# Small products and fillers in another order, other bank rings, and the LayerNorm's affine step spread over two engines, in a hybrid trunk kernel

## What is computed

```python
for layer in range(DEPTH):                       # DEPTH = 2
    mix = _even_mixer(x, ...) if layer % 2 == 0 else _odd_mixer(x, ...)
    x = _layer_norm(ALPHA * x + mix, ln1_g[layer], ln1_b[layer])
    x = _layer_norm(ALPHA * x + _swiglu(x, ...), ln2_g[layer], ln2_b[layer])

def _layer_norm(x, g, b):                        # over the last axis
    xc = x - mean(x)
    return xc * rsqrt(mean(xc * xc) + LN_EPS) * g + b

# gated linear attention, chunks of 64 tokens: the masked product within a chunk
attn = where(causal, einsum('bhcid,bhcjd->bhcij', q_g, k_g), 0.0)
o_intra = einsum('bhcij,bhcjv->bhciv', attn, vc)
# odd layer: gated RMSNorm of the delta rule's output
o = _rms_norm(o) * norm_g * silu(gate)
```

## Time and profile before

| | us |
|---|---|
| median of 3 runs | 1285.34 |
| lowest and highest | 1285.04, 1287.56 |
| the profiled execution | 1283.91 |
| its span | 1282.1 |
| TensorE busy | 1250.3 |
| VectorE, ScalarE, GpSimd busy | 462.7, 432.9, 598.9 |

### The profile page before, as it was taken

How to read it: one execution, slowest core, us unless ns; L and a number is a source line. 1 busy time by engine, 2 the same in 40 slices (tenths; PEclk the granted TensorE clock), 3 DMA queues, 4 the chain that set the end, 5 groups by cost and what they waited for, 6 DMA issues and landing times.

```text
span 1282.1 us, 16970 instructions
## 1 busy us (share of the span) xinstructions
PE 1250.3 (98%) x7104; PEld 1027.5 (80%) x7104; DVE 462.7 (36%) x763; ACT 432.9 (34%) x600; POOL 598.9 (47%) x286
## 2 busy tenths in 40 slices
PE   9999999999999999998999999999999999999997
PEld 7878877888888888886777878887788888888885
DVE  5548945211111000115687955553521101010105
ACT  4174623322222221224453355452422222221111
POOL 4241243964444443445743346364595444435341
PEclk9999999999999999999999999999999999999999
DMA  9321032333333233231344342022233333324221
GB/s 305 99 67 66 1 115 84 99 99 99 98 99 99 83 121 125 99 96 49 98 110 124 99 100 92 26 67 99 66 99 99 99 99 99 99 82 134 80 99 65
DMA packets 109375, 122.98 MB, mean 96 GB/s; under 512 B 22386, under 2 KB 84148, under 8 KB 109300
## 3 DMA queue, kind: packets, MB, share of 16 engines
q1 hardware_dynamic: 101828, 118.59, 29.4%
q10 hardware_dynamic: 7472, 3.31, 1.0%
HBM read 117.96 MB, written 3.70 MB: 95 GB/s over the span
## 4 chain that ended last, share of the span: by engine, by line
PE 86%; DVE 7%; POOL 3%; issue 3%; DVEq 1%; ACT 1%; ACTq 0%; POOLq 0%
PE bank L1562 26%; PE bank L1563 26%; PE bank L1564 26%; PE bank L1893 3%; POOL w_lo L638 2%; DVE f_ab L1083 1%; DVE KH L1355 1%; DVE OO L1333 1%; DVE SS L1331 1%; PE bank L1608 1%; DVEq L435 1%; PE bank L1721 0%; PE bank L1845 0%; DVE x_tm L1106 0%; PE bank L1782 0%
## 5 line engine op out<-in xcount | busy, mean ns | idle before, releaser
L638 POOL TENSOR_TENSOR w_lo<-w_raw,w_hi 128x1024 fp32r<-128x1024 f32 (+1 forms) x200 | 470.0, 2374 | 495.3 <-ACT w_hi L768 495.3
L1562 PE MATMUL bank<-x_hi,w_hi 128*128 128x512 f32 x928 | 364.3, 393 | 7.5 <-DVE f_ab L1083 4.0
L1564 PE MATMUL bank<-x_hi,w_lo 128*128 128x512 f32 x928 | 361.7, 390 | 0.0
L1563 PE MATMUL bank<-x_lo,w_hi 128*128 128x512 f32 x928 | 361.6, 390 | 0.0
L768 ACT ACTIVATE w_hi<-w_raw 128x1024 fp32r<-128x1024 f32 (+1 forms) x200 | 196.3, 1031 | 218.3 <-issue 167.3
L1562 PEld LDWEIGHTS bank<-x_hi,w_hi 128*128 128x128 f32 x928 | 174.6, 188 | 46.9 <-issue 8.4
L1564 PEld LDWEIGHTS bank<-x_hi,w_lo 128*128 128x128 f32 x928 | 174.5, 188 | 36.6
L1563 PEld LDWEIGHTS bank<-x_lo,w_hi 128*128 128x128 f32 x928 | 174.5, 188 | 35.4
L1150 DVE TENSOR_TENSOR f_ab<-bank,f_ab 128x512 f32<-128x512 f32 x44 | 30.4, 691 | 368.9 <-PE bank L1564 368.9
L1563 PE MATMUL bank<-w_lo,h_hi 128*128 128x512 f32 x352 | 140.4, 399 | 0.0
L1562 PE MATMUL bank<-w_hi,h_hi 128*128 128x512 f32 x352 | 138.7, 394 | 0.0
(11 more groups left out here) (270 smaller groups left out, 1179.5 us busy)
## 6 DMA issues: line engine op xcount, KB each, us to landing
w_raw<-ffn_w_gate_dram SPq DMA_DIRECT2D x22, 1024.0 KB, 5.3
w_raw<-ffn_w_up_dram SPq DMA_DIRECT2D x22, 1024.0 KB, 5.3
w_raw<-ffn_w_down_dram SPq DMA_DIRECT2D x20, 1024.0 KB, 5.0
w_raw<-od_w_in_dram SPq DMA_DIRECT2D x16, 1024.0 KB, 5.9
w_raw<-ev_w_in_dram SPq DMA_DIRECT2D x8, 1024.0 KB, 5.9
w_raw<-ev_w_out_dram SPq DMA_DIRECT2D x4, 1024.0 KB, 5.1
w_raw<-od_w_out_dram SPq DMA_DIRECT2D x4, 1024.0 KB, 5.1
x_fm<-x_fm_dram SPq DMA_DIRECT2D x8, 256.0 KB, 6.7
```

The lines of the kernel that those rows point to most:

```text
L638: pool.tensor_tensor(w_lo[:, b % 2, c], w_raw[:, b % 2, c], w_hi[:, b % 2, c].bitcast(F32), ALU.subtract).then_inc(w_lo_ready, 1)
L1562: pe.matmul(out_ap, st[0], mv_[0], start=start, stop=False)
L1563: pe.matmul(out_ap, st[0], mv_[1], start=False, stop=False)
L1564: return pe.matmul(out_ap, st[1], mv_[0], start=False, stop=stop)
```

## The change

**Even layer.** `gattn` becomes eight products of 64 by 64, both chunks of a head in the same 64 columns of the bank; `g_at` and `upto` shrink to half, and the product of `g_at` with `g_v` becomes eight of 64 rows. Six of the eight steps k of filler `gr` stay ahead of `gattn`, and two go behind the second `gstate` (in tile 0 one, and the last behind `probT`). `turn_o` of the tile before goes ahead of `sout`. The wait for the last `g_v` goes from the stage's start to the first state product. In the tail both `mix` tiles go through the first block of weights before the second, and two more tiles of `mix` follow the last `turn_o`.

**LayerNorm.** The normalisation is two instructions of 512 elements. In `round_x` ScalarE takes gain and bias for even k straight from the bank, once into `x_hi` and once into `f_ab`; VectorE does odd k and all eight `x_lo`; GpSimd's `low_parts` is gone. `fm_block` runs for each k the four passes that need `x_hi` alone, then waits for `x_lo`, then two.

**Odd layer.** The ring of banks changes at `ba_fm` instead of at the first convolution block, and two later rings are others. `ba` and what follows it move one channel later. In tile 0 the filler of place 0 goes between `kTM` and `vTM`; in the others `qk` goes between `m1` and `ds`. For the last tile VectorE does scale and gate in one (four instructions for each half), and the tail's `mix` steps are interleaved by weight block.

The core of the diff (the table of rings, the two LayerNorm parts and the even order):

```diff
-        if key == ("conv", CONV_ORDER[0]):
+        if key == ("ba_fm",):
             ring, turn = list(range(6)), 0
...
         elif key == FILLERS[0, -1]:
-            ring, turn = [0, 1, 2, 3, 6, 7, 4, 5], 0
+            ring, turn = [0, 6, 7, 1, 2, 3, 4, 5], 0
+        elif key == TAIL_FILLERS[1][0]:
+            free = [slots[k][0] for k in (("ds", NT - 1, 64), ("oT", 1, NT - 2, 0), ("oT", 1, NT - 2, 1))]
+            ring, turn = free + [b for b in ring if b not in free], 0
...
-                if b in turned:
-                    low_parts(turned[b])
...
-                for k in range(KD):
-                    taken(act, ("xT", i, k))
-                    act.activation(x_hi[:, k, :], f_ab[:, k % 4, :], ACT.Copy).then_inc(s["x_hi_ready"], 1)
+                for k in range(0, KD, 2):
+                    full(act, ("xT", i, k))
+                    act.activation(x_hi[:, k, :], src, ACT.Identity, scale=g, bias=v).then_inc(s["x_hi_ready"], 1)
+                    if k >= 4:
+                        low_part_there(act, i, k - 4)
+                    take(act.activation(f_ab[:, k % 4, :], src, ACT.Identity, scale=g, bias=v), ("xT", i, k))
+                    taken(act, ("xT", i, k + 1))
+                    act.activation(x_hi[:, k + 1, :], f_ab[:, (k + 1) % 4, :], ACT.Copy).then_inc(s["x_hi_ready"], 1)
...
-                    if k % 2:
-                        low(k - 1)
+                    if k > 1:
+                        low(k - 2)
+                    low(k - 1)
+                low(KD - 1)
...
-                    dve.tensor_scalar(x_tm[:, t, :], x_tm[:, t, :], mv[:, t, 0:1], rstd[:, t:t + 1],
-                                      ALU.subtract, ALU.mult).then_inc(s["z_norm"], 1)
+                    for h in range(2):
+                        c = slice(h * 512, (h + 1) * 512)
+                        dve.tensor_scalar(x_tm[:, t, c], x_tm[:, t, c], mv[:, t, 0:1], rstd[:, t:t + 1],
+                                          ALU.subtract, ALU.mult).then_inc(s["z_norm"], 1)
...
-                tile_of(("gr", t))
+                for key in EVEN_FILLERS[t]:
+                    tile_of(key, 0, 6)
...
+                for key in EVEN_FILLERS[t]:
+                    tile_of(key, 6, 8 if t else 7)
...
+            last = ("mix", 0, 0, NT - 1)
+            for k0 in (0, 4):
+                for key in TAIL_FILLERS[0]:
+                    tile_of(key, k0, k0 + 4)
             turn_o(0, NT - 1)
+            for k0 in (0, 4):
+                for key in LAST_FILLERS[0] + [last]:
+                    tile_of(key, k0, k0 + 4)
...
                 for hg in H:
                     per_head(("kTM", t, hg), lambda o, h: pe.transpose(o, qkv[:, KD + h, tc_], eye[:, :]))
                 filler(t, -1, 4, 8)
+                filler(t, 0)
                 if t == 0:
                     pe.wait_ge(s["conv_silu"], len(CONV_ORDER))
...
             out_square_sum(NT - 1)
+            link(dve.reciprocal(oms[:, :], oms[:, :]))
             for hg in range(2):
-                out_scale(NT - 1, hg)
+                for h in range(4 * hg, 4 * hg + 4):
+                    ins = dve.scalar_tensor_tensor(OO[:, h, :], OO[:, h, :], oms[:, h:h + 1],
+                                                   gate_s[:, NT - 1, h * P:(h + 1) * P], ALU.mult, ALU.mult)
```

More of the change, by code:

```diff
@@ L165 @@
            (3, 1): ("mix", 1, 0, 0), (3, 3): ("mix", 1, 0, 1)}
+EVEN_FILLERS = [[("gr", t)] for t in range(NT)]
 TAIL_FILLERS = {0: [("mix", 0, 0, 0), ("mix", 0, 0, 1)], 1: [("mix", 1, 0, 2)]}
-FILLED = set(FILLERS.values()) | set(TAIL_FILLERS[0]) | set(TAIL_FILLERS[1])
+LAST_FILLERS = {0: [("mix", 0, 0, 2)], 1: []}
+FILLED = set(FILLERS.values()) | set(TAIL_FILLERS[0] + TAIL_FILLERS[1] + LAST_FILLERS[0])
 OG_ORDER = [FILLERS[k] for k in sorted(FILLERS) if FILLERS[k][0] == "og"]
@@ L639, in split_lo @@
                                        ALU.subtract).then_inc(w_lo_ready, 1)
[L641 to L646, removed]
             split_lo(1)
@@ L1076, in low @@
                        .then_inc(s[("x_lo_even", "x_lo_odd")[k % 2]], 1)
-                for k in range(KD):
+                for k in range(1, KD, 2):
                     full(dve, ("xT", i, k))
@@ L1301, in _ @@
             round_o(0, NT - 1)
+            for key in LAST_FILLERS[0]:
+                add_sublayer(1, *key)
             layer_norm(1, "mix", 0)
@@ L1666, in tile_of @@
                               k == 0, k == KD - 1)
+                if key[0] == "mix" and key[-1] == NT - 1 and k1 == 4:
+                    ins.then_inc(w_used, 1)
                 if k1 == KD:
@@ L1700, in have @@
                     taken(pe, ("oT", layer, NT - 1, k // 4))
-                for half in range(2):
-                    tiles = [t for t in range(NT) if ("mix", layer, half, t) not in FILLED]
-                    tm_group(("mix", layer, half), have, in_turn=half == 1, tiles=tiles)
+                tm_group(("mix", layer, 1), have, in_turn=True)
                 turn_x(2 * layer + 1)
@@ L1807, in _ @@
                 for h in range(GH):
-                    ins = pe.matmul(go[:, h * GDV:(h + 1) * GDV], g_at[:, h, :], g_v[:, t, h * GDV:(h + 1) * GDV],
-                                    start=False, stop=h == GH - 1, skip_group_check=True)
+                    for c in range(2):
+                        rows = slice(c * CH, (c + 1) * CH)
+                        ins = pe.matmul(go[rows, h * GDV:(h + 1) * GDV], g_at[rows, h, :], g_v[rows, t, h * GDV:(h + 1) * GDV],
+                                        start=False, stop=h == GH - 1, skip_group_check=True)
                 done(ins, ("gout", t))
@@ L1967, in _ @@
                 filler(t, 2, 4, 6)
-                filler(t, 3, 0, 6)
+                held = (0, 6, 8) if t < NT - 1 else (0, 5, 7)
+                filler(t, 3, *held[0:2])
                 if t:
@@ L1991, in _ @@
                 filler(t, 2, 7, 8)
-                filler(t, 3, 6, 8)
+                filler(t, 3, *held[1:3])
                 for hg in H:
@@ L2004, in _ @@
                     per_head(("kv", t, hg), lambda o, h: mul(o, KH[:, h, :], EE[:, h, :]))
-            for key in TAIL_FILLERS[1]:
-                tile_of(key)
+            ahead, last = TAIL_FILLERS[1][0], ("mix", 1, 0, NT - 1)
+            filler(NT - 1, 3, 7, 8)
+            tile_of(ahead, 0, 4)
             turn_o(1, NT - 1)
+            tile_of(ahead, 4, 7)
+            tile_of(last, 0, 4)
+            tile_of(ahead, 7, 8)
+            tile_of(last, 4, 8)
             mix_and_norm(1)
```

99 lines of the change are left out of this document (62 added, 37 removed).

## The result

The changed kernel took 1297.12 us, median of 4 runs (1295.61 to 1298.57), against 1285.19 of the kernel before (1284.97 to 1287.56): 1.0088 of its time, 95% interval 1.0071 to 1.0106. It is slower by 12 us. Forecast was slower by 4.8, 1290.1, in a range that ended at 1295.

What follows compares the result with a forecast made beforehand. TensorE was taken as the bound, working 1250.3 of 1282.1 us. Even layer -4.0, odd layer -2.6 and LayerNorms +5.0, +5.0 and +1.4 sum to +4.8 us on 1285.34, so 1290.1 us; 8-in-10 range 1269 to 1295.

Steps and rivals of the forecast that it cites:

- The odd layer's term: Odd layer: shorter waits before kTM, qk covering GA, and the fused last gate; -2.6 us, bounds -0.5 and -4.
- the move of the ring: Second LayerNorm: the first convolution block's 3.55 us wait for f_ab and its slow passes go; -5.4 us there without a collision.
- The 0.65 ahead of the inverse's blocks: Odd tile 0: of the 3.19 us wait before kTM, 0.65 us is kept as gain; the inverse's blocks then set the pace.
- the -1.35 and -0.6: Odd tiles: qk between m1 and ds covers waits for GA, 1.35 us; the fused last gate with split order gains 0.6.
- The collision: LayerNorms: GpSimd's w_lo and affine steps take turns with VectorE's z and x_lo; +5.0, +1.4, +5.0 us at the three.
- rival 2: LayerNorms: GpSimd's first piece starts before z(3)'s first half, +6.5 us twice and +2.9 at the second; 1294.6 us, chance 0.13.
- The clock, its other half: Part of the GpSimd-first rival: idle TensorE may lose clock at the LayerNorms, 1.3 us each; thrice, 1294 from the forecast too.
- The collision-free gain: LayerNorms if nothing collided: ScalarE makes x_hi(0) from the bank, first passes start near 212.4; -1.5 us at first and third.
- The even layer: Even tiles -1.6 us (cheaper gattn, hidden waits) and even tail -2.4 (waits for w_lo and x_lo gone): -4.0 in all.
- No collision: LayerNorms: VectorE gets through before GpSimd, or GpSimd is held back; -15.0 us in all, 1270.3, chance 0.23.
- half a collision: LayerNorms: only the two w_lo come between, +2.0 us twice and -1.8 at the second; 1280.9 us, chance 0.12.
- The odd order's misfire: Odd layer: og(0,1) moved ahead waits for w_lo, a loss of 2 us; 1294 with the collision, 1274 without; chance 0.04.

Runs made afterwards that it cites:

- the first experiment: Changed kernel with its ring of six banks at ba_fm starting as 2, 3, 4, 5, 0, 1: 1288.21 us, 1.0028 of the kernel before.
- the better ring: The six-bank ring at ba_fm starting as 2, 3, 4, 5, 0, 1; alone on the changed kernel 1288.21 us, also kept in several later runs.
- both edits: Changed kernel with the six-bank ring starting as 2, 3, 4, 5, 0, 1 and GpSimd waiting for each LayerNorm's last x_lo: 1272.77 us, 0.9893 of before.
- The experiment with the filler: On top of both edits, odd tile 0's filler og(0,1) stands behind vTM again, as in the kernel before: 1272.61 us.
- The holding of GpSimd: Changed kernel, but GpSimd waits for a LayerNorm's last two x_lo before making the next block's w_lo: 1281.11 us, 0.9967 of before.
- the banks swapped: On top of both edits, xT of k = 1 gets its bank ahead of k = 0: 1271.64 us.
- only the affine step held: Changed kernel, but only GpSimd's first multiplication with ln_rows on x_tm waits for the last x_lo; the two w_lo run unheld: 1292.48 us.

## Why the prediction was wrong

**The odd layer's term is what failed.** The prediction counted the move of the ring to `ba_fm` only where it begins, at the second LayerNorm (-5.4 without a collision), and gave the rest of the odd layer -2.6, bounds -0.5 and -4. It did not follow the ring to its next restart at the 13th block. There it cost 5.42 us of waiting and some 2.4 of half clock, 8.9 in the whole kernel by the first experiment, and the stage came out at +7.35. All this could be worked out from the code: the bank of each result is a short list, and VectorE's 9.3 us of other work ahead of that block were in the trace of before. With 8.9 added, 1290.1 would have been 1299.0 for 1297.1. The other way round, with the ring alone put right the kernel took 1288.21, 3.3 over the kernel before, where the prediction had 4.8.

**The remaining odd terms: right in sign, half in size.** With the better ring, from `ba_fm` to the third turn the kernel takes 303.7 us against 304.9: -1.3 for -2.6. The 0.65 ahead of the inverse's blocks did not come. The line of before for their first product is

```profile
759.26 0.69 PE L1893 MATMUL bank<-blocks_in,GA 32*32 32x32 f32 x32
```

that is 126.35 us after TensorE starts on `decay`; with both edits it is 126.51, although `kTM` starts 3.2 us earlier, counted the same way. The experiment with the filler says that its new place saves 0.75 against the old one within the changed kernel; what of the change takes that back is not shown. Behind this product the kernel before took 144.4 us to the third turn, and the kernel with both edits 142.7: -1.7 for the -1.35 and -0.6 forecast. From `ba_fm` to `decay` it lost 0.3 (34.53 for 34.19).

**The collision: right, in place and size.** The turns of the earlier trace rows carried over as they stood. Forecast +5.0, +1.4, +5.0; measured +4.74, +0.75, +4.40, together 1.5 less. The holding of GpSimd shows it as the cause, not only as a fitting story: same instructions on VectorE, other durations. The moments came within 1.1 us too, counted from the turn, each a little earlier than forecast (z's second half, then `w_lo`, `x_lo(0)`, L732, `x_lo(1)`, L735, `x_lo(2)`), and the race at 0.1 us went the forecast's way: z's first half came first, so rival 2's GpSimd-first order did not occur. Nor did GpSimd's second piece pass by order of issue. The clock, its other half, fell at the third, where a window shows 0.91 for 1.00 before, and not at the first; at the second it is 0.90, as in the kernel before. The third stage is no longer than the first for it (+4.40, +4.74).

**The collision-free gain: too large.** 1.5 per LayerNorm was 0.9. The two Identity activations ahead of the first `x_lo` take 0.78 and 0.77 us, where 0.60 was put for one from a bank, and the prediction let the first pass start when the first of them was done; with GpSimd held it starts 5.95 us after the turn, for 4.75 forecast (212.4 less 207.65). The bank alone is not the reason: with the banks swapped the pass comes earlier and the stage gains 0.1. That the two durations explain the rest is argued and not shown. No table load came for Identity: ScalarE's `f_ab` follows `x_hi` without one, so what the Trainium skill (ScalarE: Activation LUTs, "Table sets: the hidden batching unit") states of identity agrees with this trace.

**The even layer: right.** -4.57 for -4.0. `gattn` takes 0.61 (0.58 forecast), the intra product 1.02 (1.00 before), the waits for `s_pT` in tiles 1 to 3 are gone and the one in tile 0 is 1.46 (1.5 in the sum, 1.2 in the list of signs). The tail ended the wait of the earlier trace rows.

**Rivals.** No collision, and half a collision, fell with the first trace. The odd order's misfire was given 0.04, by another mechanism: a wait for `w_lo`. That wait came, with 1.45 and 0.67 us, and stands in the profile with both edits too, so it is no part of the 8.9. No rival named the banks.

## What to carry to other kernels

When a ring of buffers is restarted or shifted, write out who precedes whom in each buffer all the way to the next restart; the place where it hurts may be a dozen results later, as here. When work is taken from one engine, look at what it does with the free time: here GpSimd used it at once for work that nobody needed yet, and blocked VectorE. A wait ahead of that work turned the loss of the whole change, 12 us, into a gain of 4. Two repairs of a few lines made the change as a whole worth 1.1% (1.0% against the 1285.19 us of the first result).

## What the runs showed of the hardware

VectorE and GpSimd exchanged turns instruction by instruction, even when GpSimd's next was queued without a wait. Those of VectorE's instructions at the LayerNorms that read and write SBUF alone (z's halves and `x_lo`) lost up to 2.2 us, nearly one whole instruction of GpSimd's (2.40): an `x_lo` took up to 2.87 us in place of 0.68. `f_ab`, which reads a bank, kept 0.81 in all 12 cases. The Trainium skill (SBUF — State Buffer, "Who interferes with whom") states that whoever issues first gets the shared port pair for the whole instruction while the other blocks; these waits of up to 2.2 us agree with that.

The clock did not follow the amount of waiting here. At the first LayerNorm of the changed kernel TensorE waited four times, 1.83, 1.14, 1.16 and 1.12 us, and its granted clock stayed at 1.00 from 209 to 226. With only the affine step held it waited 1.83 and 1.14 there and no more, and the granted clock was 0.79 on the mean from 208.5 to 224.5: the passes behind the second wait stand at half clock. Which waits tip it these runs don't show.

Runs of one kernel scatter by 3 us here, and one likely source is visible: `dec_rows_out`, a transfer on which VectorE waits in the convolutions. In the run with the banks swapped VectorE waited 6.1 us for it, and TensorE 1.5 for what follows. With both edits alone VectorE waited 2.3 us for it and TensorE not at all. From `decay` to `kTM` the profiles with the better ring fall into two groups: 105.8 us in four of them (waits of VectorE's of 1.8 to 2.5 us), 107.5 to 107.8 in three (5.8 to 6.1). Why the transfer lands late is not shown, and no kernel was profiled in both ways.

```profile
645.70 1.29 DVE L1411 TENSOR_TENSOR EE<-EE,GU 128x512 f32<-128x512 f32 x2 [6.10 <-DMA GU<-dec_rows_out]
...
655.50 0.33 PE L1897 MATMUL bank<-qkv 128*32 128x32 f32 x16 [1.53 <-DVE GT L1422]
```
